# A two-layer hybrid decoder trunk: setup joined with the first layer, modulation sums by block turns, and the last norm turned and scaled by rows

## The chip, the cores and the metric

The kernel runs on one core of one Trainium2 chip. The metric is the device time of one execution in microseconds (us). A profiled execution gives, beside its time, a trace of every engine: TensorE (PE, with its weight loads as PEld), VectorE (DVE), ScalarE (ACT), GpSimd (POOL), SyncE (SP) and the DMA queues.

## What is computed

The reference, cut to what matters here (512 tokens, width 1024, two layers, all in float32):

```python
c_act = jax.nn.silu(c)
for l in range(DEPTH):
    mod = c_act @ ada_w[l] + ada_b[l]                      # 1024 -> 9 * 1024
    sh1, sc1, g1, sh2, sc2, g2, sh3, sc3, g3 = jnp.split(mod, N_MOD, axis=-1)
    h = modulate(rms_norm(x, ffn1_norm[l]), sh1, sc1)      # y * (1 + sc) + sh
    x = x + 0.5 * g1[:, None, :] * swiglu(h, ffn1_w_in[l], ffn1_w_out[l])
    h = modulate(rms_norm(x, mix_norm[l]), sh2, sc2)
    ...                                                    # attention and convolution branches
    x = x + g2[:, None, :] * (merged @ w_mix_out[l])
    h = modulate(rms_norm(x, ffn2_norm[l]), sh3, sc3)
    x = x + 0.5 * g3[:, None, :] * swiglu(h, ffn2_w_in[l], ffn2_w_out[l])
return rms_norm(x, final_norm)
```

The attention adds a bias that depends on the distance of two tokens (a table of 8 heads by 32 buckets) and uses a scalar lambda per layer, made of four vectors of 64.

## The kernel before

x is kept in SBUF with channels on the partitions: 8 tiles (j) of 128 channels by 512 tokens (`x_res`). Each matrix product is done in float32 accuracy with three reduced-precision products: a weight slab of 128 output channels is loaded by SP (`w_raw`, `slab`, L285), rounded by ACT (`w_hi_part`, L390), its rest taken by DVE (`w_lo_part`, L680), and PE runs, for each of its 8 (or 6) chunks, three matmuls of 512 columns, high by high, high by low, low by high (`slab`, L1205). There are two slots for slabs. The order of the work on each engine is written out by hand, and semaphores tie the engines together.

**Norms.** A norm's scale per token is not known when the product with x can start. So a stage's first two slabs (`two_slabs`, L1220) are multiplied with x times a per-channel scale, without the token's factor, and their result is scaled afterwards (`read_bank` in `norm_units`, L722); two columns with the shift are multiplied in the same pass (L1240, L1241). Meanwhile PE sums the squares over channels (`norm_mean`, L1263, a matmul with a constant matrix), ACT takes the root (L396) and DVE the reciprocal (L692). `norm_units` then makes the 8 normed tiles on DVE and ACT, and the second pair of slabs and all later ones use those.

**Modulation.** The product of the activated c with `ada_w` runs on DVE, beside the matmuls: for each chunk of 1024 outputs, 8 weight tiles of 128 by 1024 are multiplied by one scalar per partition and added (`ada_step`, L784). What is left is a sum over the 128 partitions. `chunk_parts` (L797) splits the 128 by 1024 sum into a high and a low part, `mod_sum_parts` (L1275) adds over partitions with four matmuls of 512 columns, `mod_rows` (L804) copies the two rows out, `mod_turn` (L1285) turns them into columns with four float32 matmuls, which the trace shows as eight, and `mod_columns` (L810) adds `ada_b`. There are 16 such chunks, 8 in input stages of feed-forward networks (ffn), 8 in output stages; POOL's queue loads their weights (`ada_chunk`, L356).

**Setup (L293 to L484, L828 to L880, L1293 to L1329).** The first two chunks of layer 0 (shift and scale of the first norm) come as 8 loads of 1 MB on POOL's queue into `ada_first`. SP loads x by rows and 16 small parameter rows, then the first weight slabs. ACT's queue issues the loads of c, convolution taps, bias table and eight broadcasts of the lambda vectors, before ACT activates c (L450). PE turns x tile by tile (L1302), ACT copies and squares each tile, DVE adds the squares. Eight rows of the attention bias are made, one per head, each replicated over 128 partitions (L1316, L1317), copied (L468, L469) and written to HBM (L472). PE then adds the first chunks over partitions (L1271) and turns them (L1289), DVE makes the scale and shift columns, and the first norm's pass starts (L1237).

**End.** In the last ffn's output stage (L953 to L978) each of 8 channel tiles takes three slabs; DVE updates x (L776), ACT squares it (L435), DVE adds the square (L782). After the last tile follow the mean over channels (L1261), root, reciprocal of 128 by 512 (L694), 8 times a scaled tile (L1199), four PE turns (L1502) and an ACT copy (L673), and eight stores of 256 KB (L333), the second four behind the last copy.

## Time and profile before

| | us |
|---|---|
| time, median of 3 runs | 2619.57 (2619.23 to 2621.32) |
| time of the profiled execution | 2620.49 |
| its span in the trace | 2618.7 |
| PE busy | 2558.0 (98%) |
| DVE busy | 1669.3 (64%) |
| ACT busy | 973.8 (37%) |
| POOL busy | 101.3 (4%) |

The profiled execution is 0.92 us over the median of the runs, and its own span is 1.8 us shorter than its time. PE's busy time counts every moment in which some matmul is in flight; matmuls overlap, so a full PE is read from the pitch between their starts. A float32 matmul stands in the trace as two.

### The profile page before, as it was taken

How to read it: one execution, taken by the hardware profiler on the slowest of the kernel's cores; microseconds unless marked ns; L12 is line 12 of the kernel's file. 1: busy time of each engine (PE TensorE's matmuls, PEld its weight loads, DVE VectorE, ACT ScalarE, POOL GpSimd, SP SyncE). 2: the span in 40 equal slices, each digit the busy share in tenths (PEclk: the TensorE clock that was granted, in tenths of full speed). 3: DMA queues.
4: the chain of work that ended last, by engine and by line, in shares of the span. 5: the costliest groups of instructions: out<-in, count | busy, mean ns of one | idle time of the engine just before them, and what ended most of it. 6: DMA issues, size and time to landing. Idle time of an engine off the chain costs nothing.

```text
span 2618.7 us, 34873 instructions
## 1 busy us (share of the span) xinstructions
PE 2558.0 (98%) x11578; PEld 2059.3 (79%) x11578; DVE 1669.3 (64%) x2449; ACT 973.8 (37%) x1637; POOL 101.3 (4%) x163
## 2 busy tenths in 40 slices
PE   4999999999999999999999999999999999999997
PEld 2688888777778888888878888877777788788886
DVE  3655567789898666544365556678898875633333
ACT  2422222554554433222232222244554453422222
POOL 0000001000000000000000001101000000000000
PEclk9999999999999999999999999999999999999998
DMA  6355556232223344543324556632222333333332
GB/s 225 113 156 160 160 185 216 77 88 84 80 84 90 94 125 122 159 128 92 96 85 139 150 159 195 222 101 85 80 84 80 93 93 93 91 96 97 98 95 92
DMA packets 469953, 311.96 MB, mean 119 GB/s; under 512 B 11047, under 2 KB 447529, under 8 KB 468872
## 3 DMA queue, kind: packets, MB, share of 16 engines
q1 hardware_dynamic: 445260, 227.69, 29.8%
q0 software_dynamic: 19584, 75.51, 8.5%
q10 hardware_dynamic: 5052, 8.02, 1.0%
q8 instruction: 34, 0.56, 0.1%
q14 instruction: 23, 0.19, 0.0%
HBM read 306.13 MB, written 5.05 MB: 119 GB/s over the span
## 4 chain that ended last, share of the span: by engine, by line
PE 93%; DVE 4%; ACT 1%; ACTq 1%; issue 1%; DVEq 0%
PE bank L1215 28%; PE bank L1217 27%; PE bank L1216 27%; PE bank L1413 2%; PE bank L1392 1%; PE bank L1242 1%; ACTq L446 1%; PE bank L1237 1%; PE bank L1238 1%; DVE rstd L694 1%; PE bank L1384 1%; DVE w_lo L683 1%; PE bank L1289 1%; DVE scaled L705 1%; PE bank L1316 1%
## 5 line engine op out<-in xcount | busy, mean ns | idle before, releaser
L683 DVE TENSOR_TENSOR w_lo<-w_raw,w_hi 128x1024 fp32r<-128x1024 f32 (+1 forms) x434 | 522.4, 1204 | 578.2 <-ACT w_hi L394 577.6
L1215 PE MATMUL bank<-h_hi,w_hi 128*128 128x512 f32 x2112 | 838.7, 397 | 0.0
L1217 PE MATMUL bank<-h_hi,w_lo 128*128 128x512 f32 x2112 | 823.8, 390 | 0.0
L1216 PE MATMUL bank<-h_lo,w_hi 128*128 128x512 f32 x2112 | 822.2, 389 | 0.0
L394 ACT ACTIVATE w_hi<-w_raw 128x1024 fp32r<-128x1024 f32 (+1 forms) x434 | 451.7, 1041 | 878.3 <-PE bank L1217 866.8
L1215 PEld LDWEIGHTS bank<-h_hi,w_hi 128*128 128x128 f32 x2112 | 396.5, 188 | 89.7 <-issue 8.2
L1217 PEld LDWEIGHTS bank<-h_hi,w_lo 128*128 128x128 f32 x2112 | 396.4, 188 | 84.6
L1216 PEld LDWEIGHTS bank<-h_lo,w_hi 128*128 128x128 f32 x2112 | 397.0, 188 | 77.9 <-issue 0.5
L1005 DVE SCALAR_TENSOR_TENSOR conv_part<-glu,conv_taps,conv_part 128x512 f32<-128x512 f32 x464 | 318.9, 745 | 0.0
L1215 PE MATMUL bank<-s_hi,w_hi 128*128 128x512 f32 x704 | 274.6, 390 | 0.0
L1217 PE MATMUL bank<-s_hi,w_lo 128*128 128x512 f32 x704 | 274.0, 389 | 0.0
L1216 PE MATMUL bank<-s_lo,w_hi 128*128 128x512 f32 x704 | 273.9, 389 | 0.0
L1215 PEld LDWEIGHTS bank<-s_hi,w_hi 128*128 128x128 f32 x704 | 132.1, 188 | 27.7
L1217 PEld LDWEIGHTS bank<-s_hi,w_lo 128*128 128x128 f32 x704 | 132.1, 188 | 27.5
L1216 PEld LDWEIGHTS bank<-s_lo,w_hi 128*128 128x128 f32 x704 | 132.2, 188 | 27.4
L793 DVE SCALAR_TENSOR_TENSOR ada_acc<-ada_raw,c_act,ada_acc 128x1024 f32<-128x1024 f32 x112 | 143.4, 1280 | 0.9
L364 POOL DMA_DIRECT2D ada_raw<-in_ada_w x128 | 67.9, 531 | 1270.2 <-DVE ada_acc L790 575.2
L513 ACT ACTIVATE s_hi<-full 128x512 f32 (+1 forms) x84 | 53.1, 632 | 166.3 <-DVE full L916 166.3
L918 DVE TENSOR_TENSOR s_lo<-full,s_hi 128x512 f32 (+1 forms) x84 | 58.2, 693 | 75.3 <-ACT s_hi L513 75.3
L435 ACT ACTIVATE squares<-x_res 128x512 f32 x48 | 30.3, 632 | 197.3 <-DVE x_res L776 197.3
L569 ACT ACTIVATE probs<-probs,neg_row_max 128x512 f32<-128x512 f32 (+3 forms) x128 | 71.0, 556 | 76.7 <-DVE neg_row_max L1042 76.6
L782 DVE TENSOR_TENSOR running_sum<-running_sum,squares 128x512 f32<-128x512 f32 x56 | 38.8, 692 | 78.8 <-ACT squares L435 44.1
(182 smaller groups left out, 2642.3 us busy)
## 6 DMA issues: line engine op xcount, KB each, us to landing
w_raw<-in_ffn_w_in SPq DMA_DIRECT2D x176, 512.0 KB, 3.8
ada_raw<-in_ada_w POOLq DMA_DIRECT2D x128, 512.0 KB, 4.7
w_raw<-in_w_mix_in SPq DMA_DIRECT2D x112, 512.0 KB, 3.6
w_raw<-in_ffn_w_out SPq DMA_DIRECT2D x64, 512.0 KB, 3.9
w_raw<-in_ffn_w_out SPq DMA_DIRECT2D x32, 384.0 KB, 3.4
w_raw<-in_w_mix_out SPq DMA_DIRECT2D x18, 512.0 KB, 3.8
ada_first<-in_ada_w POOLq DMA_DIRECT2D x8, 1024.0 KB, 24.3
w_raw<-in_w_attn_branch SPq DMA_DIRECT2D x16, 512.0 KB, 3.8
```

The lines of the kernel that those rows point to most:

```text
L364: pool.dma_start(ada_raw[k % 4][:, :], w_ada[:, ds(layer * KT + k, 1), ds(m * D, D)].rearrange("p o f -> p (o f)"))\
L394: act.activation(whi[slot][:, 0:n, :], raw[slot][:, 0:n, :], ACT.Copy).then_inc(w_hi[slot], 1)
L513: act.activation(tile(SHI2, i), F[0][:, :], ACT.Copy).then_inc(sem("s_hi"), 1)
L569: act.activation(PR[par][m][:, 0:n], PR[par][m][:, 0:n], ACT.Exp, bias=nmx[:, par, m:m + 1], scale=-1.0, accum_out=rsum[:, par, m:m + 1]). ...
L683: dve.tensor_tensor(wlo[slot][:, 0:n, :], raw[slot][:, 0:n, :], whi[slot][:, 0:n, :].bitcast(F32), ALU.subtract).then_inc(w_lo[slot], 1)
L793: ins = dve.scalar_tensor_tensor(out=ACC[:, :], in0=ada_raw[k % 4][:, :], scalar=CA[:, k:k + 1], in1=ACC[:, :], op0=ALU.mult, op1=ALU.add)
L918: dve.tensor_tensor(tile(SLO2, i), F[0][:, :], tile(SHI2, i).bitcast(F32), ALU.subtract)\
L1005: ins = dve.scalar_tensor_tensor(out=CAB[t % 2][:, :], in0=Z[:, t:t + TOK], scalar=wt, in1=CAB[t % 2][:, :], op0=ALU.mult, op1=ALU.add)
L1215: pe.matmul(acc, wh, hi[:, k0 + k, :], start=first and k == 0, stop=False)
L1216: pe.matmul(acc, wh, lo[:, k0 + k, :], start=False, stop=False)
L1217: mm = pe.matmul(acc, wl, hi[:, k0 + k, :], start=False, stop=last and k == n - 1)
L1413: mm = pe.matmul(S[m][:, 0:n], QT[m * HD:(m + 1) * HD, i * P:(i + 1) * P], KTT[m * HD:(m + 1) * HD, 0:n], start=True, stop=True)
```

## The change

- `ada_w`'s first 2 MB by 4 are loaded in two halves, the scale's 8 tiles first; the shift's 8 tiles and the lambda broadcasts follow on POOL's queue once the first two weight slabs have landed. SP loads the small rows before x.
- All bias rows come from one pair of matmuls (16 partitions per head) and are written by eight stores, issued by ACT after it has made the first high parts.
- The squares of x are summed along x's rows by ACT, and put into `running_sum` as scaled columns of the identity matrix.
- The first pass of slabs starts when the scale is known. Its shift columns are multiplied after it (`late`), the mean of squares at its ninth step.
- Each chunk's sum over partitions is made by turning 32 by 32 blocks on DVE, a reduction of each block's rows on DVE, and one float32 matmul of 32 columns; four small additions give the columns.
- In the last stage, x times `final_norm` is turned tile by tile between slabs, squares are summed per token by matmuls of one column, and at the end row blocks are scaled once and stored in four stores of 512 KB. The last stage's loop is written out.
- The lambda sums and exponentials move behind the first norm and the first ffn's input stage.

```diff
-    TBX = at("table_wide", [P, HEADS, P], F32, s0 + 4256)
+    TBX = at("table_wide", [P, HEADS, P // HEADS], F32, s0 + 4256)
@@ block.sync
-        for t in range(QB):
-            sp.dma_start(XS[:, t, :], a["x"][0, t * P:(t + 1) * P, :]).then_inc(sem(f"x_in{t}"), 16)
         for l in range(DEPTH):
...
+        for t in range(QB):
+            sp.dma_start(XS[:, t, :], a["x"][0, t * P:(t + 1) * P, :]).then_inc(sem(f"x_in{t}"), 16)
...
+        for n in range(QB):
+            t = n // 2 + 2 * (n % 2)
+            sp.wait_ge(sem(("y_scaled_dve", "y_scaled_act")[n % 2]), n // 2 + 1)
+            sp.dma_start(out[0, t * P:(t + 1) * P, :], YO[:, t, :]).then_inc(sem("y_out"), 16)
@@ block.gpsimd
         for k in range(KT):
-            pool.dma_start(ADA0[:, k, :], w_ada[:, k, 0:2 * D]).then_inc(sem(f"ada0_in{k}"), 16)
+            pool.dma_start(ADA0[:, k, D:2 * D], w_ada[:, k, D:2 * D]).then_inc(sem(f"ada0_scale{k}"), 16)
+        for s in range(2):
+            pool.wait_ge(w_raw[s], 16)
+        for k in range(KT):
+            pool.dma_start(ADA0[:, k, 0:D], w_ada[:, k, 0:D]).then_inc(sem(f"ada0_shift{k}"), 16)
+        for l in range(DEPTH):
+            for n, name in enumerate(("lambda_q1", "lambda_k1", "lambda_q2", "lambda_k2")):
+                pool.dma_start(LV[:, l, n, :], bass.AP(a[name].tensor, l * HD, [[0, P], [1, HD]]))\
+                    .then_inc(sem("lambda_in"), 16)
@@ block.scalar
+        act.activation(BR[:, 0:TOK], TP[1][:, :], ACT.Copy).then_inc(sem("br_copied"), 1)
+        act.activation(BR[:, TOK:TOK + P], TP[0][:, 0:P], ACT.Copy).then_inc(sem("br_copied"), 1)
         for j in range(KT):
             act.wait_ge(sem("xp_ready"), j + 1)
             act.activation(X[:, j, :], bank[2 + j % 2][:, :], ACT.Copy).then_inc(sem("x_ready"), 1)
-            act.wait_ge(sem("ssum_add"), j)
-            act.activation(SQ[:, :], bank[2 + j % 2][:, :], ACT.Square).then_inc(sem("sq_ready"), 1)
+        for t in range(QB):
+            act.activation(JUNK[t % 2][:, :], XS[:, t, :], ACT.Square, accum_out=row_sq[:, t:t + 1])...
...
         for s in range(2):
             w_hi_part(0, s)
+        for t in range(QB):
+            act.activation(SSUM[:, t * P:(t + 1) * P], ident[:, :], ACT.Copy, scale=row_sq[:, t:t + 1])...
         for j in range(KT):
             plain_hi(0, j)
+        for c in range(HEADS):
+            act.dma_start(bass.AP(src.tensor, src.offset + c * (P // HEADS) * (TOK + P),
+                          [[P * (TOK + P), HEADS], [TOK + P, P // HEADS], [1, TOK + P]]), BR[:, :])...
@@ block.vector
         def chunk_parts(seq):
             dve.wait_ge(sem("ada_step"), (seq + 1) * KT)
-            dve.tensor_copy(ACCH[:, :], ACC[:, :]).then_inc(sem("acc_hi"), 1)
-            dve.wait_ge(sem("acc_hi"), seq + 1)
-            dve.tensor_tensor(ACCL[:, :], ACC[:, :], ACCH[:, :].bitcast(F32), ALU.subtract).then_inc(sem("acc_parts"), 1)
+            dve.transpose(ACCT[:, :], ACC[:, :]).then_inc(sem("acc_turned"), 1)
+            dve.wait_ge(sem("acc_turned"), seq + 1)
+            dve.wait_ge(sem("mod_summed"), seq + 1)
+            dve.tensor_reduce(RED[:, :], ACCT[:, :].rearrange("p (b r) -> p b r", r=32), AX.X, ALU.add)\
+                .then_inc(sem("acc_parts"), 1)
+        def chunk_columns(layer, hc, turn):
+            dve.wait_ge(sem("mod_summed"), turn + 1)
+            for q in range(4):
+                quarter = slice(q * 32, (q + 1) * 32)
+                ins = dve.tensor_tensor(MODC[quarter, ...], O[quarter, q:D // 32:4], PT[quarter, ...], ALU.add)
+            ins.then_inc(sem("modc_ready"), 1)
...
         for k in range(KT):
+            first_step(1, "scale", k)
+        first_parts(1, 0)
...
+        w_lo_part(0, 0)
+        w_lo_part(0, 1)
+        dve.wait_ge(sem("scale0_summed"), 1)
+        quarter_columns(KT).then_inc(sem("scale0_ready"), 1)
         scale_columns(0, 0).then_inc(sem("ac_ready"), 1)
-        shift_columns(0, 0)
         for j in range(KT):
             plain_lo(0, j)
+        for k in range(KT):
+            first_step(0, "shift", k)
+        first_parts(0, 1)
+        dve.wait_ge(sem("mod_summed"), 1)
+        quarter_columns(0).then_inc(sem("modc_ready"), 1)
+        shift_columns(0, 0)
...
+        dve.tensor_copy(YO[:, :, j * P:(j + 1) * P], TP[j % 2]...)
+        dve.reciprocal(yrstd[:, :], yroot[:, :]).then_inc(sem("y_rstd"), 1)
+        for t in (0, 1):
+            dve.tensor_scalar(YO[:, t, :], YO[:, t, :], yrstd[:, t:t + 1], None, ALU.mult)...
@@ block.tensor
+            if late:
+                pe.wait_ge(sem("scale0_ready"), 1)
+                first_sum(1).then_inc(sem("mod_summed"), 1)
+                pe.wait_ge(sem("shift_parts"), 2)
+                for slot in range(2):
+                    for n in range(KT):
+                        wh, wl = whi[slot][:, n, :], wlo[slot][:, n, :]
+                        pe.matmul(S[slot][:, 0:2], wh, SHP[:, shift, n, :], start=n == 0, stop=False)
+                        mm = pe.matmul(S[slot][:, 0:2], wl, SHP[:, shift, n, :], start=False, stop=n == KT - 1)
+                    mm.then_inc(w_used[slot], 1)
+        def turn_rows(j):
+            pe.wait_ge(sem("y_gained"), j + 1)
...
+            for t in range(QB):
+                mm = pe.transpose(TP[j % 2][:, t * P:(t + 1) * P], T[j % 2][:, t * P:(t + 1) * P], ident[:, :])
+        def token_sums():
+            for t in range(QB):
+                pe.matmul(AUX[:, t:t + 1], SSUM[:, t * P:(t + 1) * P], invd[:, 0:1], start=t == 0, stop=False)
         def mod_sum_parts(turn):
-            for r in range(2):
-                one = SELR[:, ROWS_MAX - 1 - r:ROWS_MAX - 1 - r + 64]
-                pe.matmul(O[0:64, :], one, ACCH[:, r * TOK:(r + 1) * TOK], start=(r == 0), stop=False)
-                mm = pe.matmul(O[0:64, :], one, ACCL[:, r * TOK:(r + 1) * TOK], start=False, stop=(r == 1))
+            pe.matmul(O[:, 0:D // 32], SELG[:, :], RED[:, :], start=True, stop=True).then_inc(sem("mod_summed"), 1)
-        def mod_turn(turn, rows):
-            for q in range(4):
-                mm = pe.matmul(O[:, q:4 * rows:4], MR[0:64, q * P:(q + 1) * P], ident[0:64, 0:rows], ...)
```

## Rows read from the trace of the kernel before

**Rows 1.** Page, part 4: the chain that ended last, by engine

```profile
PE 93%; DVE 4%; ACT 1%; ACTq 1%; issue 1%; DVEq 0%
```

**Rows 2.** Timeline, 0 to 110 us: start, duration, engine, line, operation, count, wait before

```profile
9.21 20.39 SPq L287 DMA_DIRECT2D w_raw<-in_ffn_w_in  x2
...
16.19 1.33 PE L1302 MATMUL bank<-ident,x_rows 128*128 128x128 f32 x5 [4.82 <-DMA x_rows<-in_x]
...
19.66 3.68 ACTq L446 DMA_DIRECT2D lambda_rows<-in_lambda_k  x1
...
23.85 10.61 ACTq L446 DMA_DIRECT2D lambda_rows<-in_lambda_k  x1
...
43.85 1.12 PE L1302 MATMUL bank<-ident,x_rows 128*128 128x128 f32 x4 [0.24 <-ACT squares L456]
...
78.73 0.77 PE L1237 MATMUL bank<-h_hi,w_hi 128*128 128x512 f32 x1 [3.85 <-DVE h_lo L771]
...
86.63 3.35 DVE L694 RECIPROCAL rstd<-rstd 128x512 f32<-128x512 f32 x1 [3.15 <-ACT rstd L401]
...
95.79 1.22 DVE L683 TENSOR_TENSOR w_lo<-w_raw,w_hi 128x1024 fp32r<-128x1024 f32 x1
...
109.47 0.47 PE L1215 MATMUL bank<-h_hi,w_hi 128*128 128x512 f32 x1
```

**Rows 3.** The tile ada_first's eight loads: time from issue to landing

```profile
DMA to landing us min/median/max: 11.0/24.3/35.1
```

**Rows 4.** Windows: stretch, length, PE, PEld, DVE, ACT, POOL, PEclk, DMA share, GB/s

```profile
25.00:30.00 5.00, 0.00 (x0) 0.00 (x0) 0.00 (x0) 0.00 (x0) 0.00 (x0) 1.00 1.02 388
...
82.00:86.00 4.00, 4.00 (x10) 2.59 (x10) 1.48 (x6) 0.16 (x1) 0.00 (x0) 0.55 0.91 264
86.00:90.00 4.00, 4.00 (x25) 3.43 (x23) 3.35 (x1) 0.53 (x1) 0.00 (x0) 1.00 0.03 10
```

**Rows 5.** Page, part 5: groups, with busy time and mean ns of one

```profile
L394 ACT ACTIVATE w_hi<-w_raw 128x1024 fp32r<-128x1024 f32 (+1 forms) x434 | 451.7, 1041 | 878.3 <-PE bank L1217 866.8
...
L793 DVE SCALAR_TENSOR_TENSOR ada_acc<-ada_raw,c_act,ada_acc 128x1024 f32<-128x1024 f32 x112 | 143.4, 1280 | 0.9
```

**Rows 6.** Timeline around one chunk's sum and turn, ffn input stage

```profile
170.71 1.22 DVE L802 TENSOR_TENSOR ada_acc_lo<-ada_acc,ada_acc_hi 128x1024 fp32r<-128x1024 f32 x1
...
174.85 0.39 PE L1281 MATMUL bank<-ada_acc_hi,row_select_r 128*64 128x512 f32 x1
...
175.76 0.39 PE L1215 MATMUL bank<-h_hi,w_hi 128*128 128x512 f32 x1
...
186.41 0.39 PE L1217 MATMUL bank<-h_hi,w_lo 128*128 128x512 f32 x1
...
188.04 0.40 PE L1216 MATMUL bank<-h_lo,w_hi 128*128 128x512 f32 x1
```

**Rows 7.** Timeline of PE: one turn (at 552) and a mean (at 464) between matmuls

```profile
552.25 0.39 PE L1217 MATMUL bank<-h_hi,w_lo 128*128 128x512 f32 x1
...
552.82 0.39 PE L1216 MATMUL bank<-h_lo,w_hi 128*128 128x512 f32 x1
...
464.17 0.48 PE L1242 MATMUL bank<-h_hi,w_lo 128*128 128x512 f32 x1
...
465.57 0.39 PE L1238 MATMUL bank<-h_lo,w_hi 128*128 128x512 f32 x1
```

**Rows 8.** Timeline around one chunk's sum, ffn output stage

```profile
422.64 0.69 DVE L800 CAST ada_acc_hi<-ada_acc 128x1024 fp32r<-128x1024 f32 x1
423.37 1.23 DVE L802 TENSOR_TENSOR ada_acc_lo<-ada_acc,ada_acc_hi 128x1024 fp32r<-128x1024 f32 x1
...
424.88 0.39 PE L1281 MATMUL bank<-ada_acc_hi,row_select_r 128*64 128x512 f32 x1
```

**Rows 9.** Timeline of the end

```profile
2597.32 0.75 DVE L776 SCALAR_TENSOR_TENSOR x_res<-bank,gates,x_res 128x512 f32 x1 [1.93 <-PE bank L1217]
...
2610.84 5.21 SPq L333 DMA_DIRECT2D out<-y_rows  x8
```

More of the change, by code:

```diff
@@ L1218, in slab, with two_slabs @@
             mm.then_inc(w_used[slot], 1)
[L1220 removed]
+        def two_slabs(pair, use, ready, shift=None, at={}, banks=G, late=False):
             lag = 4
@@ L1238, in two_slabs @@
                     pe.matmul(acc, wh, HLO[:, n, :], start=False, stop=False)
-                    if shift is not None:
+                    if shift is not None and not late:
                         pe.matmul(S[slot][:, 0:2], wh, SHP[:, shift, n, :], start=n == 0, stop=False)
@@ L1368, in _ @@
                              k0, OUTG[g], g == 0, g == 2,
-                             at={2: lambda: mod_sum_parts(seq + 1)} if w == 0 and m == 5 else {})
-                    if w == 0:
-                        mod_turn(seq + 1, 2)
+                             at=extra.get(m, {}))
+                if last:
+                    for i in range(KT // 2):
+                        out_pair(i)
+                else:
+                    with pe.Fori(0, KT // 2) as i:
+                        out_pair(i)
                 if w == 1:
```

351 lines of the change are left out of this document (191 added, 160 removed).

## The prediction

> **What bounds the kernel now.** I read the chain of waits first: 93% of the path that ended last is PE [rows 1]. Inside the stages PE takes a 512-column matmul every 0.2275 us: four of them in 0.91 us [rows 6]. So two kinds of time can be won: matmuls that are not the product itself, and the two ends in which PE waits. The timeline of the start shows the first: the pass of the first norm begins at 78.73 us, and only at 109.47 us do the plain slabs begin [rows 2]. The first 35 us go to ACT's queue, which is stuck in issuing lambda loads (the last takes 10.61 us, to 34.5), so c is not activated before that. The timeline of the end shows the second: the last update of x starts at 2597.32 us of a span of 2618.7, 21.4 us from the end [rows 9]. Between them, 16 chunk sums interrupt PE.
>
> **The chunk sums.** Removed on PE, per chunk: four matmuls, 0.91 us, and the turn. Around the turn two matmul starts that are normally 0.455 us apart stand 188.04 - 186.41 = 1.63 us apart [rows 6], so it costs 1.18 us. Together 2.09 us. Added: one float32 matmul of 32 columns, two in the trace. The trace has none of this form. The nearest rows are a single 128-column turn, which stretches two starts from 0.455 to 0.57 us, so 0.12 us, and the mean with two float32 passes of 512 columns, 1.40 - 0.455 = 0.95 us [rows 7]. I take 0.3 us, twice the turn's price and a little for the start, since the short form is much nearer to the turn. Per chunk 1.8 us, for 16 chunks 29 us; by the ends 31.5 and 18.2 us.
>
> On DVE, a copy of 0.69 us and a subtraction of 1.23 us, 1.95 us with the gap [rows 8], give way to a block turn and a reduction of 128 by 1024. Neither operation is in the trace. The cheapest pass of that width is the copy, 0.69 us; the dearest DVE operation is the reciprocal, 3.35 us for 512 columns, 6.7 us for 1024 [rows 2]. Most passes of that width take 1.2 to 1.3 us [rows 5, 8]. I take 1.2 us for each, since both read every column once: 2.4 us, 0.5 us more than now. In the input stage the low part ends at 171.93 and PE asks at 174.85 [rows 6], so 2.9 us of other matmuls hide it. In the output stage it ends at 424.60 and PE asks at 424.88 [rows 8]: only 0.28 us. There PE will wait some 0.25 us in each of 8 chunks, 2 us. The row copy that goes and the four small additions that come lie on neither path; behind them on DVE stands the next slab's low part, which is early there. Net gain of this part: 27 us.
>
> The Trainium skill (VectorE: DVE Perf Modes, The perf-mode tier table) states that the reduction runs in the slowest mode, one element per cycle, and (Vector Engine (DVE) Microarchitecture Reference, The reshape front-end and per-opcode configuration) that the block turn also sustains one element per cycle. By both the pair would take an estimated 2.2 us, and PE's wait in the output stage would all but vanish; no row here shows either.
>
> **The setup.** ACT's queue keeps only six issues, so c is active before 10 us and this delay is gone. What comes next? *Transfers.* The start moves data at 388 GB/s [rows 4]. Before the shift half come 4.2 MB of scale weights, 2.1 MB of x, 1.05 MB of slabs and 0.3 MB of taps and tables: 20 us of full rate. But x is now issued behind the 16 small rows, just ahead of the slabs' issue at 9.21 us, where before it landed by 16.2 us [rows 2], and it shares the rate with the scale loads. With half the rate it needs 11 us from about 8.5; the last load of a group also lags (one took 35.1 us from its issue [rows 3]). I put x's landing at 25 us (20 to 27) and the last scale tile at 31.
>
> *The chain from x.* Eight tiles turn at 1.1 us (the 1.12 us of four turns [rows 2]), and the copy ends at 34.5. ACT then squares four rows of 1024 columns (1.04 us each as its own pass of that width [rows 5], and some 0.1 for the sum read out): 39.1; taps 39.8; high parts of both slabs 41.9. DVE's second low part ends at 43.1 (1.22 us), four additions and the scale column at 44. Then one high part (0.65), one low part (0.7), and PE's first matmul stands at 45.5 us, against 78.73. The scale's own chain is shorter: its last step at 31 + 1.3, turn, reduction and matmul by 36, hidden behind ACT.
>
> *The chain of the shift.* This is where gain is given back. DVE's eight low parts end at 50.2 (0.7 us each, a little under the 0.75 us of a like pass [rows 9], since passes overlap). Only then does it start on eight shift steps, 0.7 + 7 x 1.28 = 9.7 us [rows 5]: 59.9. Their loads are issued once the slabs have landed, about 35, and need 11 us: hidden. Turn and reduction 62.3, PE's matmul and the columns 63.7. In the same DVE order stands the reciprocal, which before began at 86.63. PE has ended its pass by 60, 16 matmuls at about 0.43 and 32 at 0.23 us plus the mean; it waits until 62, does the sum and, at 64, 32 shift matmuls in some 4 us, and waits again: the second pass needs a low part that stands 10.4 us behind the reciprocal's start (95.79 + 1.22 - 86.63 [rows 2]), so it starts at 74.2. From the reciprocal's start to the plain slabs it was 109.47 - 86.63 = 22.8 us; the lambda sums, now in between on DVE, add 0.8: 87.4.
>
> At 74.2 PE comes from some 6 idle us. After such a stretch before the first pass, the granted clock was 0.55 between 82 and 86 us and 1.00 between 86 and 90 [rows 4], that is 1.2 GHz at first and 2.4 GHz then; the first pass began at 78.73, so some 7 us went at 1.2 GHz. I charge 5 to 7 us at half speed, which puts 48 matmuls at 13 to 14.5 us and the plain slabs at 88.2. The Trainium skill (TensorE: Matmul & The Clock Gate, HAM oscillation) says that an idle stretch sends the clock back to half; this trace agrees, with the 0.55 just named. With a clock that stayed up DVE's chain would decide, and the plain slabs would stand at 87.4. Gain of the setup: 109.47 - 88.2 = 21.3 us. Its bounds: x by 20 us gives 26; by 27 us and a second pass wholly at half speed (48 x 0.43 = 20.6 us from 76) gives 13.
>
> The 8 stores of bias rows are costed at nothing: ACT issues them from 50 us on, and its next task, the root, is wanted at 60. If that cover goes, the second rival below has the price. Chunk loads on POOL's queue wait for the lambda sums, at 82; the first of them is wanted when the first chunk's tile begins, near 98: hidden. SP's slabs of the second pair are issued at 41 and share the rate with the shift loads until 50; they are wanted at 70.
>
> **The end.** Added to PE in the last stage: seven groups of four turns at four times 0.12 us [rows 7], 3.4 us, and four float32 matmuls of one column, eight in the trace, at no more than the removed turn's 1.18 us [rows 6], 1.0. ACT's products and copies (half a slab's 1.04 us [rows 5] and a little, 0.6 us each) lie in its idle time; the slab behind them is needed a whole slab later. After PE's last matmul, taken as 0: x updated at 1.0; square 1.85; column sums 3.0; last product by ACT 2.4, turned 3.8; a dummy high part and a copy keep ACT until 3.9, the root is there at 4.3; DVE's dummy low part ends at 4.7, the last copy 5.4, the reciprocal of four columns 5.6. Scaling: DVE 6.3 and 7.0, ACT 6.7 and 7.7. The first store's data flows from 7.7, 2.1 MB at 388 GB/s [rows 4] take 5.4 us, and the end comes at 14. Now it is 21.6 us (0.25 us from PE's last matmul to 2597.32, then 21.4). Gain 7.6 - 4.4 = 3 us, between -2 and 6.
>
> **Sum.** 27 + 21.3 + 3 = 51.3 us off the profiled execution's 2620.5: 2569.2. The median of the runs is 0.9 lower: 2568. A change of 0.2%, about 5 us, is what a measurement of this kernel can tell from none.
>
> **Rivals.** (1) *The block turn is slow on DVE.* If it costs what the reciprocal does per column (6.7 us, with the reduction 7.9, 6.0 more than now), PE waits 6.0 - 2.9 = 3.1 us in 8 input-stage chunks and 5.7 in 8 output-stage ones, 70 us in all, and 5.5 more in the shift's chain. Against 53.3 us of gain without waits this gives 2619.6 + 22 = 2642: slower. It decides from a block turn of about 5.4 us on. For it: a turn over partitions is no ordinary pass. Against: no other DVE row here is as slow per column as the reciprocal. The page on the microarchitecture named above speaks against it. Chance 4%.
>
> (2) *ACT is caught in issuing stores.* Eight stores back to back on its queue, as the lambda loads were, of which the last two took 3.68 and 10.61 us to issue [rows 2]. At 3.5 us each ACT is free at 78 instead of 53; the root then is 19 us later, the reciprocal at 79.5 instead of 63.8, and 15.7 us of the setup's gain are gone: 2584. For it: the same queue, 128 packets each. Against: those loads were issued while the queues moved 388 GB/s [rows 4]; by 50 us most loads have landed. Chance 14%.
>
> (3) *The sum matmul costs as much as a mean* (0.95 us), and DVE's pair is half a us longer than I think: 18.2 - 6 = 12 us instead of 27: 2583. Chance 12%.
>
> (4) *The early start does not come*, because the slabs land as late as 41 us, as the 35.1 us of the slowest load of the start allow [rows 3]: ACT's high parts end at 43 and the shift loads flow until 58; the plain slabs begin near 91: 2571, inside the forecast's range. The part that would not do what it says is the shift, which ends up as long as all of the old setup; at most 21 us, 2589. Chance of the latter 4%.
>
> **Numbers.** Forecast case 66%, on its own 2556 to 2579; the rivals 14, 12, 4 and 4%. The range of 2554 to 2587 takes in the rivals at 2583 and 2584 and the faster bounds of clock, x and matmul. Faster by over 0.2%: 94%; within 0.2%: 2%; slower: 4%.
>
> **What would show it.** First matmul of the first norm near 45.5 us; plain slabs near 88; between them two gaps on PE, 60 to 62 and 68 to 74, with a low granted clock behind the second. Chunk pairs in the output stage about 1.6 us shorter, each with a short PE wait on the reduction; input-stage groups 1.8 us shorter with no wait. Block turn and reduction near 1.2 us each. Last matmul to the end 14 us. Wrong would be: PE waiting for the reduction by more than 0.5 us, ACT's root behind store issues, or x landing after 30 us.

## The result, and where the time went

The kernel after took 2576.5 us (median of 4 runs, 2575.4 to 2577.8), the kernel before 2619.4 beside it (2618.6 to 2621.3): ratio 0.9835, 95% interval 0.9818 to 0.9852. The forecast was 2568, its range 2554 to 2587. The sum was 51.3 us of gain, and 42.9 came. The profiled execution took 2577.0 us, its span is 2575.3.

An update of x is the same instruction in both kernels, so the difference of its start times cuts the gain into parts. First the updates of the kernel before, from the timeline of DVE (start, duration, engine, line, operation, tiles, idle time before it), the first of the first output stage and the first of the last one:

```profile
349.46 0.75 DVE L776 SCALAR_TENSOR_TENSOR x_res<-bank,gates,x_res 128x512 f32 x1
...
2492.62 0.75 DVE L776 SCALAR_TENSOR_TENSOR x_res<-bank,gates,x_res 128x512 f32 x1 [1.94 <-PE bank L1217]
```

And those of the kernel after, with the last update of all (before, it is the first line of [rows 9]):

```profile
327.18 0.74 DVE L810 SCALAR_TENSOR_TENSOR x_res<-bank,gates,x_res 128x512 f32 x1
...
2453.25 0.75 DVE L810 SCALAR_TENSOR_TENSOR x_res<-bank,gates,x_res 128x512 f32<-128x512 f32 x1 [1.70 <-PE bank L1292]
...
2562.38 0.75 DVE L810 SCALAR_TENSOR_TENSOR x_res<-bank,gates,x_res 128x512 f32<-128x512 f32 x1 [2.64 <-PE bank L1292]
```

The lead is 22.3 us at the first of them and 39.4 at the second. At the last it is only 2597.32 - 2562.38 = 34.9: the last stage gives 4.4 back. At the end of the span it is 43.4. With the plain slabs' start (109.47 in [rows 2], 92.03 below) the gain splits into **setup 17.4, chunk sums 21.9, end 4.0** (8.5 behind the last update, less 4.4). The forecast had 21.3, 27 and 3.

**The setup.** The timeline of the kernel after, 20 to 92 us:

```profile
22.62 0.47 PE L1399 MATMUL bank<-ident,x_rows 128*128 128x128 f32 x1 [14.55 <-DMA x_rows<-in_x]
...
30.10 0.48 PE L1399 MATMUL bank<-ident,x_rows 128*128 128x128 f32 x1 [3.18 <-DMA x_rows<-in_x]
...
31.96 4.48 PE L1399 MATMUL bank<-ident,x_rows 128*128 128x128 f32 x21 [1.38 <-DMA x_rows<-in_x]
35.44 4.18 POOL L355 DMA_DIRECT2D ada_first<-in_ada_w  x8 [29.25 <-DMA w_raw<-in_ffn_w_in]
49.06 0.77 PE L1312 MATMUL bank<-h_hi,w_hi 128*128 128x512 f32 x1 [9.63 <-DVE h_lo L805]
...
66.62 0.61 PE L1375 MATMUL bank<-ada_group_sums,group_select 128*128 128x32 f32 x2 [3.77 <-DVE ada_group_sums L846]
...
68.27 3.35 DVE L728 RECIPROCAL rstd<-rstd 128x512 f32<-128x512 f32 x1
...
78.87 0.77 PE L1312 MATMUL bank<-h_hi,w_hi 128*128 128x512 f32 x1 [3.47 <-issue]
...
92.03 0.47 PE L1290 MATMUL bank<-h_hi,w_hi 128*128 128x512 f32 x1
```

The four tiles of x land one by one, the last at 31.95 us and not at 25. PE's first matmul stands at 49.06 (forecast 45.5, before 78.73), the reciprocal at 68.27 (63.8), the second pass 10.6 us behind it (10.4), the plain slabs at 92.03 (88.2). The windows of the kernel after (stretch, length, PE, PEld, DVE, ACT, POOL busy, PEclk, DMA share, GB/s) hold the reason for x and a second surprise:

```profile
25.00:30.00 5.00, 0.47 (x1) 0.18 (x1) 2.13 (x2) 0.00 (x0) 0.00 (x0) 1.00 0.34 103
30.00:35.00 5.00, 3.52 (x15) 2.62 (x16) 3.62 (x3) 1.80 (x3) 0.00 (x0) 1.00 0.14 42
...
70.00:75.00 5.00, 5.00 (x25) 5.00 (x25) 4.73 (x6) 1.48 (x3) 0.00 (x0) 0.50 0.00 0
75.00:80.00 5.00, 1.53 (x5) 1.29 (x6) 4.93 (x8) 3.12 (x4) 0.00 (x0) 0.50 0.00 1
```

PE, ACT and POOL wait for loads from 25 us on (PE and ACT up to 32, POOL up to 35.44), and yet the sixteen DMA engines are a third, then a seventh busy. And the clock is at its lower level, 1.2 GHz, from 70 to 80 us, in the first half of it with PE never idle: the 32 shift matmuls of 2 columns took 7.0 us where I had put 4.

**The chunk sums.** In the input stage, the timeline of PE in the kernel after: the sum's two matmuls between plain ones, and, 11 us later, the loop's turning point:

```profile
157.17 0.40 PE L1292 MATMUL bank<-h_hi,w_lo 128*128 128x512 f32 x1
157.40 0.31 PE L1381 MATMUL bank<-ada_group_sums,group_select 128*128 128x32 f32 x2
157.54 0.48 PE L1290 MATMUL bank<-h_hi,w_hi 128*128 128x512 f32 x1
157.86 0.39 PE L1291 MATMUL bank<-h_lo,w_hi 128*128 128x512 f32 x1
...
168.29 0.39 PE L1292 MATMUL bank<-h_hi,w_lo 128*128 128x512 f32 x1
168.70 0.47 PE L1290 MATMUL bank<-h_hi,w_hi 128*128 128x512 f32 x1
169.00 0.39 PE L1291 MATMUL bank<-h_lo,w_hi 128*128 128x512 f32 x1
```

From 157.17 to 157.86 are two steps, normally 0.455, so the sum costs 0.24 us (forecast 0.3). From 168.29 to 169.00 it is 0.26 more than two steps, with nothing in between: here PE's loop over the chunks starts over. At its second turn, at 234.11, it is 0.3 more; where the loop ends, at 300.01, only 0.1. Before, the modulation turn stood at this very place ([rows 6], up to 188.04), and any such time was part of its 1.18 us. In the output stage:

```profile
368.26 1.22 DVE L837 TENSOR_REDUCE ada_group_sums<-ada_acc_turned 128x32 f32<-128x1024 f32 x1
...
368.87 0.39 PE L1292 MATMUL bank<-s_hi,w_lo 128*128 128x512 f32 x1
...
369.53 0.41 PE L1381 MATMUL bank<-ada_group_sums,group_select 128*128 128x32 f32 x2 [0.27 <-DVE ada_group_sums L837]
...
370.09 0.40 PE L1291 MATMUL bank<-s_lo,w_hi 128*128 128x512 f32 x1
```

PE could go on at 369.10, the reduction ends at 369.48: from 368.87 to 370.09 is 1.22 us, 0.77 over two steps. Less the 0.24 of the sum itself, 0.53 go to the wait (0.38 up to the end of the reduction) and to the start behind it. The period of a pair there (two channel tiles and one chunk) is 30.73 us (32.06 before), that of a group of six tiles with one chunk in the input stage 65.86 (67.42).

**The end.** The timeline of the kernel after, behind the last update at 2562.38:

```profile
2563.16 0.63 ACT L454 ACTIVATE squares<-x_res 128x512 f32<-128x512 f32 x1 [4.68 <-DVE x_res L810]
...
2565.45 1.22 DVE L717 TENSOR_TENSOR w_lo<-w_raw,w_hi 128x1024 fp32r<-128x1024 f32 x1 [2.33 <-ACT w_hi L401]
2566.60 0.68 DVE L1268 COPY y_rows<-bank 128x512 f32<-128x512 f32 x1
2567.41 0.18 DVE L1272 RECIPROCAL y_rstd<-y_root 128x4 f32<-128x4 f32 x1
...
2568.41 2.90 SPq L333 DMA_DIRECT2D out<-y_rows  x4
```

A reciprocal of 4 columns, 0.18 us, does what 3.35 us did, and 12.9 us lie between the last update and the end, where 21.4 lay in [rows 9].

### The profile page after: what moved, and what is told of

It reads as the page before. It is cut to its first block, busy times and chain, and to the rows that moved or that the text cites. A ratio compares the mean times of both kernels' runs of the same rounds, so it can differ in the third digit from the quotient of the medians.

```text
span 2575.3 us, 34488 instructions
## 1 busy us (share of the span) xinstructions
PE 2509.5 (97%) x11392; PEld 2032.6 (79%) x11392; DVE 1671.7 (65%) x2488; ACT 972.7 (38%) x1635; POOL 108.7 (4%) x177
## 4 chain that ended last, share of the span: by engine, by line
PE 85%; DVE 8%; ACT 3%; issue 2%; DMA 1%; SPq 0%; ACTq 0%; DVEq 0%
PE bank L1290 26%; PE bank L1292 26%; PE bank L1291 26%; PE bank L1513 2%; DVE ada_acc L827 1%; PE bank L1492 1%; ACT w_hi L401 1%; DVE rstd L728 1%; DMA x_rows<-in_x 1%; DVE w_lo L717 1%; DVE scaled L739 1%; PE bank L1312 1%; PE bank L1484 1%; DVE h_lo L748 1%; PE bank L1313 1%
## 5 line engine op out<-in xcount | busy, mean ns | idle before, releaser
L1290 PE MATMUL bank<-h_hi,w_hi 128*128 128x512 f32 x2112 | 838.9, 397 | 1.6 <-DVE scaled L963 1.3
L454 ACT ACTIVATE squares<-x_res 128x512 f32 (+1 forms) x48 | 30.4, 633 | 194.4 <-DVE x_res L810 194.4
L1312 PE MATMUL bank<-h_hi,w_hi 128*128 128x512 f32 x192 | 81.6, 425 | 17.1 <-DVE h_lo L805 9.6
```

What stands on the lines that cost most here:

```text
L1290: pe.matmul(acc, wh, hi[:, k0 + k, :], start=first and k == 0, stop=False)
L1312: pe.matmul(acc, wh, HHI[:, n, :], start=n == 0, stop=False)
```

## Experiments

The times are medians of 5 runs (of 4 in experiment 7), to be set against 2576.5. The same code moves by about 1 us between executions, so what is smaller is read in the traces, and a trace is one execution too: five kernels with the same setup, but for a few small instructions (the kernel after and those of experiments 5 to 8), have their plain slabs at 91.89 to 93.30 us.

**1. x first.**

```
+        for t in range(QB):
+            sp.dma_start(XS[:, t, :], a["x"][0, t * P:(t + 1) * P, :]).then_inc(sem(f"x_in{t}"), 16)
         for l in range(DEPTH):
             rows = [("ffn1_norm", KT), ("mix_norm", KT), ("ffn2_norm", KT), ("conv_dw_bias", KT),
...
-        for t in range(QB):
-            sp.dma_start(XS[:, t, :], a["x"][0, t * P:(t + 1) * P, :]).then_inc(sem(f"x_in{t}"), 16)
```

> The kernel after, with the four loads of x issued ahead of the 16 small rows on SP's queue. In the kernel after x lands at 31.95 us. Theory A (the forecast's: the end of the setup hangs on x through ACT and the order on DVE): x lands at 20 to 24 us, the first matmul moves from 49.06 to about 44, and the plain slabs from 92.03 to about 87: 5 us faster, 2571.5. Theory B (the shift's loads are next: POOL issues them only when the two slabs have landed, at 35.4, and DVE's last shift step already waited for its tile until 62.65): x lands early and the first matmul moves, but the shift steps end no earlier than 63.5, the plain slabs stand at 91.5 or later, and the time is within 1 us of 2576.5.

2568.5 us, 8.1 faster. x had landed by 11.9 us, and the plain slabs stood at 83.56. Theory A holds, by more than it said: the setup hangs on x, and the shift's loads (the shift steps now run from 44.7 to 55.2) were not next. The timeline and windows of this kernel show what was:

```profile
11.86 6.92 PE L1399 MATMUL bank<-ident,x_rows 128*128 128x128 f32 x32
...
30.50 1.91 PE L1408 MATMUL bank<-ident,tap_rows 31*128 31x31 f32 x16 [4.40 <-DMA tap_rows<-in_conv_dw]
...
34.26 4.17 POOL L355 DMA_DIRECT2D ada_first<-in_ada_w  x8 [28.06 <-DMA w_raw<-in_ffn_w_in]
```

```profile
25.00:30.00 5.00, 0.67 (x2) 0.29 (x2) 2.17 (x2) 0.00 (x0) 0.00 (x0) 0.50 0.06 25
30.00:35.00 5.00, 1.91 (x16) 1.78 (x16) 4.11 (x5) 2.56 (x5) 0.74 (x2) 0.50 0.05 15
```

The 31 rows of taps land only now, at 30.5 us, and up to then the DMA share is 0.06: one engine of sixteen, at 25 GB/s, while DVE waits for scale tiles and POOL for the slabs.

**2. Taps behind x.**

```
-        for l in range(DEPTH):
-            act.dma_start(CWR[0:CK, l, :], a["conv_dw"][l, :, :]).then_inc(sem("taps_in"), 16)
...
         act.activation(BR[:, TOK:TOK + P], TP[0][:, 0:P], ACT.Copy).then_inc(sem("br_copied"), 1)
+        for t in range(QB):
+            act.wait_ge(sem(f"x_in{t}"), 16)
+        for l in range(DEPTH):
+            act.dma_start(CWR[0:CK, l, :], a["conv_dw"][l, :, :]).then_inc(sem("taps_in"), 16)
```

> The kernel after, with the two tap loads (31 partitions, 124 KB each) issued on ACT's queue only when x has landed. Theory C (the taps pass through one of the 16 DMA engines or few, and x, the scale tiles and the slabs each have a part behind them there: between 25 and 35 us the DMA share is only 0.34 and 0.14, while the tiles of x land 3.2 to 3.8 us apart): without them x lands at 21 to 24 us instead of 31.95, the slabs by 26 instead of 35.4, so that the shift's loads start 9 us earlier too; the taps land 10 us after x, about 33, and ACT's high parts stand at 35 to 36; first matmul 41 to 42, plain slabs 84 to 85, 7 to 8 us faster: 2569. Theory D (x is late because it is issued late and shares the rate): the taps are 0.25 MB, 0.6 us at 388 GB/s; x lands at 31 or later, the taps after it delay ACT, and the time is 2577 to 2585.

2576.9 us, no difference, and yet theory C holds in its first half. The timeline of this kernel:

```profile
20.83 6.01 PE L1401 MATMUL bank<-ident,x_rows 128*128 128x128 f32 x29 [0.82 <-DMA x_rows<-in_x]
...
24.77 4.16 POOL L355 DMA_DIRECT2D ada_first<-in_ada_w  x8 [18.60 <-DMA w_raw<-in_ffn_w_in]
...
41.06 1.91 PE L1410 MATMUL bank<-ident,tap_rows 31*128 31x31 f32 x16 [14.02 <-DMA tap_rows<-in_conv_dw]
43.54 2.00 ACT L401 ACTIVATE w_hi<-w_raw 128x1024 fp32r<-128x1024 f32 x2
```

x is there at 20.83 instead of 31.95, the slabs at 24.77 instead of 35.44: 11 us, for 0.25 MB that were moved away. 248 KB at the 25 GB/s of one engine are 10 us. Theory D, by which the same bytes were 0.6 us, is out. What the expectation missed: the taps then took 20 us, most likely because their engine also carried its share of the shift's loads, which were issued 4 us behind them; and ACT's high parts stand behind the tap copies in its order. The gain was lost to the next wait in the same chain.

**3. Taps in 124 partitions.** The same bytes as 124 rows of 1 KB, two transposes and a rearranging copy for each layer.

```
-            act.dma_start(CWR[0:CK, l, :], a["conv_dw"][l, :, :]).then_inc(sem("taps_in"), 16)
+            act.dma_start(CWR[0:4 * CK, l, :], a["conv_dw"][l, :, :].rearrange("k (q c) -> (k q) c", q=4)).then_inc(sem("taps_in"), 16)
...
-            for h in range(HEADS):
-                mm = pe.transpose(G[l][:, h * CK:(h + 1) * CK], CWR[0:CK, l, h * P:(h + 1) * P], ident[0:CK, 0:CK])
+            for b in range(2):
+                mm = pe.transpose(G[l][:, b * 4 * CK:(b + 1) * 4 * CK], CWR[0:4 * CK, l, b * P:(b + 1) * P], ident[0:4 * CK, 0:4 * CK])
```

> The kernel after, with each tap load in 124 partitions of 1 KB rows instead of 31 of 4 KB, turned by two matmuls instead of eight; it stays where it was on ACT's queue. Theory C (the load of 31 partitions goes through one DMA engine, which the tiles of x, scale and slabs all need; the run with the taps behind x had x at 20.83 us and the slabs at 24.8, but the taps themselves only at 41.06): x lands at 20 to 23 us, the slabs by 27, the taps before both; ACT's high parts start near 32, first matmul near 38, plain slabs near 81 instead of 92: 11 us faster, 2565.5. Theory E (the spread load is slow too, or the tap turn and copies get dearer): x at 26 or later, and 0 to 6 us faster. Theory F (the early part moves, but ACT, issuing its eight stores of bias rows while the shift loads flow, has the root late): first matmul near 38, the root behind the shift steps' end, and less than 8 us faster.

2571.6 us, 4.9 faster; x at 25.52, plain slabs at 86.67. Between C and E: against the kernel with the taps away x still loses 4.7 us, where 31 rows cost it 11.1. The Trainium skill (DMA: Bandwidth & Descriptors, Why a DMA increments its semaphore by 16 and not by 1, the paragraph How many engines) says that a DMA is split over the largest number of engines, up to 16, that divides the slowest dimension of both its sides: which makes one for 31 rows, four for 124, sixteen for 128. The share of 0.06 in experiment 1 agrees with the one; the two delays agree in their order, though 4.7 is more than a quarter of 11.1.

**4. Both, and the later sum.** The edits of experiments 1, 3 and 5 together.

> The kernel after, with three edits: taps in 124 partitions, x issued first on SP's queue, the output stage's chunk sum three K tiles later. If C holds: x at 12 us as with x first alone, scale by 20 and slabs by 25, high parts from 23, first matmul near 30, shift steps from 34 to 45, plain slabs near 73, 19 us before those of the kernel after; with the 3.1 to 3.6 us of the later sum: 2554. If the shift's loads (4.2 MB, 11 us at 388 GB/s, issued at 25 beside the second slabs and the bias-row stores) are next: plain slabs at 75 to 78 and 2556 to 2559. If the taps are still what ACT waits for (30.5 us with x first alone): about 2565.

2557.4 us, 19.1 faster than the kernel after. Plain slabs at 76.61, 15.4 earlier; the sum gave the rest. Read at the same place, x first alone gave 8.5 (83.56) and the spread taps alone 5.4 (86.67): together they give 1.6 more than their sum, little beyond the 1.4 by which equal setups differ. That each alone leaves the chain to the other wait is seen in the traces: with x first ACT waits for the taps up to 32.45, with the taps spread x lands at 25.52 only.

**5. The sum three K tiles later.**

```
-                        extra[5] = {2: lambda: mod_sum_parts(seq + 1)}
+                        extra[5] = {5: lambda: mod_sum_parts(seq + 1)}
```

> The kernel after, with the chunk sum of the output stage three K tiles later in the same slab (nine matmuls, 2.0 us). In the kernel after, the output stage's pair period is 30.73 us against 29.92 for 132 matmuls at 0.2267: 0.81 per chunk, of which the sum's own slot is 0.24 by the input stage, and PE asks some 0.4 us before the reduction ends. Theory A: the wait goes, the period is 30.2, 8 chunks times 0.55: 4.4 us faster, 2572.1. Rival: the extra is no wait for the reduction but the restart of PE at a changed kind of matmul, or the wait turns up at DVE's small additions behind the slab: the period stays within 0.1 us of 30.73 and the time within 1 us of 2576.5.

2573.4 us, 3.1 faster by the medians. The pair period is now 30.17 (341.94 to 372.11), 0.56 less in each of 8 chunks, 4.5 us in all: theory A. The profile has no wait for the reduction left. Its plain slabs stood 0.6 us later than those of the kernel after (92.66), in the same code, which the total has lost.

**6. The old chunk sums in the kernel after.** DVE's copy and subtraction, PE's four matmuls and the turn, as before; setup and end stay.

> The kernel after with the chunk sums of the kernel before (copy and subtraction on DVE, four matmuls and the turn on PE; the setup and the end stay new). By the stretches between updates of x in the two traces this part gave 21.9 us, which would make it 2598.4. By the forecast it gave 27 us: 2603.5. Less than 20 would mean that part of what the stretches show belongs to the setup or to the norms' entries.

2598.4 us, 21.9 slower than the kernel after: the part's price by the stretches, but not to the tenth. In the profiled executions 21.7 us lie between the two, and 1.3 of them came before the plain slabs (93.30), in the setup that this edit hardly touches: the sums themselves cost 20.4 there. 8 chunks of the input stage at 1.56 and 8 of the output stage at 1.33 would be 23.1; see below for the rest.

**7. The old end in the kernel after.**

> The kernel after with the end of the kernel before: no turns or token sums in the last stage; mean, root and reciprocal over 512 columns, product, turn and copy tile by tile, eight stores. By the stretches of the two traces the new end costs 4.4 us in the last stage and saves 8.5 behind the last update of x, 4.0 in all: 2580.6. By the forecast 3 us: 2579.6. A difference under 2 or over 6 us would mean that the two ends interact with something else.

2582.6 us (4 runs), 6.1 slower. Its trace has 104.7 us from the first to the last update of the last stage (109.1 in the kernel after, so 4.4 is what the new end costs there) and 22.2 from the last update to the end (12.9). That makes 4.8; the rest of the 6.1 lies in the stretches ahead of the last stage, where the two kernels are the same, by 0.8 in the profiled executions. So 4 to 6 us for the new end.

**8. The tail without unused slab parts.**

```
-                        w_lo_part(p + 1, m % 2, OUTG[(m + 2) % 3] if m < 4 else 8)
+                        if not (last and i == KT // 2 - 1 and m >= 4):
+                            w_lo_part(p + 1, m % 2, OUTG[(m + 2) % 3] if m < 4 else 8)
```

ACT's high parts get the same condition, and the two loads behind them go.

> The kernel after without the slab parts that nobody uses at the end: the last two loads of w_raw, high parts and low parts. In the kernel after DVE's low part (1.22 us from 2565.45) stands in front of the copy of the last tile (2566.60), whose turn was done near 2565.7, and ACT's high part stands in front of a copy and the root. Theory A (both are on the path that ends last): from the last update of x to the end 12.92 becomes 12.0 us, 0.9 us faster. Rival (the stores' transfers decide, 339 GB/s in the last 5 us, or the root does): less than 0.3 us in that stretch. By the medians alone this is near what cannot be told.

From the last update (2563.80) to the end (2576.0) are 12.2 us instead of 12.9: most of what theory A said. The median, 2577.7, does not show it. In the profiled execution the first update of x came 0.9 us later than in the kernel after (granted clock 0.51 from 80 to 85 us, where that has 0.65) and another 0.5 was lost before the last stage, in the same code: more than what the edit gives. It is kept for its trace alone.

**9. A warm PE, first try.** Ten float32 matmuls that nobody reads, in PE's waits of the first norm.

> The kernel after, with ten float32 matmuls of 512 columns that nobody reads (running_sum by inv_d into the second pass's first bank, which that pass clears) in PE's waits around the first norm's shift: three before the sum, one behind it, four behind the shift matmuls, two more once three low parts are done. In the kernel after the granted clock is 0.50 to 0.65 between 65 and 85 us; the 32 shift matmuls take 7.0 us and the second pass 13.16 us from 78.87. Theory A (the clock costs little, since DVE's ladder ends at 86.93 whatever PE does): the clock stays near 1.00, the shift matmuls take about 3.5 us, the second pass still begins at 78.9, and the plain slabs move from 92.03 to 91 at most: 0 to 1 us faster. Theory B (PE at 1.2 GHz binds the second pass): plain slabs at 89.8, 2.2 us faster. Third case: the clock falls all the same, the idle-time matmuls run at 1.9 us each and PE is late: the plain slabs stand 5 us or more later.

2577.5 us, no difference: the third case in part. The shift matmuls, begun at a clock of 1.00, took 3.7 us instead of 7.0, but the clock fell before they were through: the last two steps between them are 0.21 us, the others 0.11 (granted 0.70 from 70 to 75, 0.62 from 75 to 80). The last fillers made the second pass 1.7 us late, at 80.58, and it then ran at full speed to 91.88.

**10. A warm PE, second try.** The same, with four of the fillers among the shift matmuls.

```
                         mm = pe.matmul(S[slot][:, 0:2], wl, SHP[:, shift, n, :], start=False, stop=n == KT - 1)
-                    mm.then_inc(w_used[slot], 1)
+                        if n % 4 == 3:
+                            if n == KT - 1:
+                                mm.then_inc(w_used[slot], 1)
+                            pe.matmul(TP[0][:, :], invd[:, :], SSUM[:, :], start=True, stop=True)
```

> The kernel after with ten float32 matmuls of 512 columns that nobody reads, placed otherwise than in the first try: three before the first norm's sum, one behind it, one after every eighth of the 32 shift matmuls, two behind them. In the first try the clock was 1.00 up to 72 us, but fell during the matmuls of 2 columns, so that the fillers behind them took 1.8 us each and the second pass began at 81.1 instead of 78.9. Theory A (wide matmuls in between hold the clock): granted clock 0.95 or more from 65 to 85 us, second pass from 78.9 at a pitch of 0.23, plain slabs at 90 to 90.6, DVE's last low part at 86.9 being what holds them; 1.5 us faster. Rival (the clock falls in any case): fillers at 1.8 us each, second pass at 80 or later, plain slabs at 92 or later.

2576.8 us, no difference. The windows of this kernel:

```profile
70.00:75.00 5.00, 5.00 (x31) 3.75 (x30) 4.73 (x6) 1.38 (x2) 0.00 (x0) 1.00 0.00 1
75.00:80.00 5.00, 3.53 (x10) 1.64 (x10) 4.93 (x8) 3.23 (x4) 0.00 (x0) 1.00 0.00 0
80.00:85.00 5.00, 4.56 (x20) 3.03 (x19) 4.93 (x8) 2.17 (x3) 0.00 (x0) 1.00 0.65 190
```

The clock stayed at 2.4 GHz, and the plain slabs moved from 92.03 to 91.41 only. Its timeline shows why:

```profile
82.72 0.39 PE L1317 MATMUL bank<-h_hi,w_lo 128*128 128x512 f32 x1
83.42 0.50 PE L1312 MATMUL bank<-h_hi,w_hi 128*128 128x512 f32 x1 [0.31 <-DVE h_lo L748]
```

A fast PE waits for DVE's low parts. Theory A holds for the clock, not for the 1.5 us: in this pair of traces 0.6 us were gained, which is less than equal setups differ by (experiment 7, without fillers, has its plain slabs at 91.89). So the clock at 1.2 GHz costs the setup little here, and how little these runs don't show.

**11. The small root.** Edits 1, 3, 5 and 8, and the first norm's root and reciprocal taken on the 128 by 4 row sums, as at the end.

```
+        act.activation(row_root[:, :], row_sq[:, :], ACT.Sqrt, bias=eps[:, 0:1], scale=1.0 / D).then_inc(sem("row_root"), 1)
...
-            act.activation(SSUM[:, t * P:(t + 1) * P], ident[:, :], ACT.Copy, scale=row_sq[:, t:t + 1]).then_inc(sem("row_sums"), 1)
+            act.activation(SSUM[:, t * P:(t + 1) * P], ident[:, :], ACT.Copy, scale=row_rstd[:, t:t + 1]).then_inc(sem("row_sums"), 1)
...
-            root(l * AUXN + AUX_NORM[k], l * UNITS + UNIT_NORM[k])
+            if l == 0 and k == 0:
+                act.wait_ge(sem("aux_ready"), 1)
+                act.activation(RSTD[:, :], AUX[:, :], ACT.Copy, scale=float(D)).then_inc(sem("aux_read"), 1)
+            else:
+                root(l * AUXN + AUX_NORM[k], l * UNITS + UNIT_NORM[k])
...
+        dve.reciprocal(row_rstd[:, :], row_root[:, :]).then_inc(sem("rstd_ready"), 1)
```

> The three edits of the 2557.4 us kernel (taps in 124 partitions, x first, later sum), the short end without unused slab parts, and one more: the first norm's root and reciprocal are taken on the 128 by 4 row sums (0.18 us as at the end) before they are spread over the bank, and DVE's reciprocal of 512 columns (3.35 us, at 53.05 there) goes. Theory A (DVE's order behind the shift binds up to the second pass): the second pass starts 3.3 us earlier, at 60.3, plain slabs at 73.3 instead of 76.6; with 0.7 at the end 4.0 us faster: 2553.4. Rival (the 32 shift matmuls at 1.2 GHz are next: they end near 60.2, and slot 1's high part and DVE's reading of the second bank wait for them): plain slabs at 74.5 or later, 2 us or less from this edit: 2555.

**2552.0 us** (2551.0 to 2553.4), ratio to the kernel before 0.9743, interval 0.9730 to 0.9756: the fastest of all, 24.5 us under the kernel after. The timeline of the kernel:

```profile
60.27 0.35 PE L1344 MATMUL bank<-shift_parts,w_lo 128*128 128x2 f32 x1
61.04 0.77 PE L1324 MATMUL bank<-h_hi,w_hi 128*128 128x512 f32 x1 [0.41 <-issue]
...
73.42 0.47 PE L1302 MATMUL bank<-h_hi,w_hi 128*128 128x512 f32 x1
```

Plain slabs at 73.42, 3.2 earlier, by theory A; but the second pass now stands right behind the last shift matmul, so the rival is next. One more row, from the timeline of ACT:

```profile
38.46 8.12 ACTq L499 DMA_DIRECT2D bias_rows<-bias_row  x2
46.63 0.60 ACT L424 ACTIVATE rstd<-bank 128x512 f32<-128x512 f32 x1 [9.51 <-issue]
```

The last two stores of bias rows hold ACT for 8.1 us while the shift's loads flow.

**12. Small root and warm PE.** Eight fillers, and none among or behind the last eight of the 32 shift matmuls.

> The 2552.0 us kernel with the unread float32 matmuls in PE's waits of the first norm: four before the sum, one behind it, and one after every eighth shift matmul but the last (three). In that kernel the 32 shift matmuls ran at 1.2 GHz, ended at 60.5 and held the second pass, which began at 61.04 and ended at 73.42. Theory A (PE is what binds there now, so that the clock has a price, other than in the kernel after): granted clock near 1.00 from 50 to 70 us, shift matmuls and fillers end near 60.4, second pass from 60.5 at full speed; DVE's last low part then holds it, plain slabs near 72: 1.0 to 1.8 us faster, 2550.6. Rival (DVE's order binds there too): plain slabs at 73.2 or later and no difference, 2552.

2554.9 us, 2.9 slower than experiment 11 (2.4 in the profiled executions): both theories missed. The windows:

```profile
55.00:60.00 5.00, 4.51 (x29) 3.41 (x27) 4.90 (x7) 3.26 (x5) 0.00 (x0) 0.99 0.25 100
60.00:65.00 5.00, 4.39 (x10) 3.51 (x11) 4.96 (x8) 2.06 (x3) 0.00 (x0) 0.50 0.37 109
```

The clock held up to 60 us and had fallen when the second pass began (at 60.60), behind eight bare shift matmuls, still 0.11 us apart, and 1.1 idle us. The pass then ran its first part at 1.2 GHz and ended at 74.50, 1.1 later. What the fall hangs on isn't settled by these runs: in experiment 10 three fillers and 1.5 idle us followed the last shift matmul and the clock held, here no filler did. The other 1.3 us came after the first update of x, in the same code.

## Why the forecast held, and where its steps failed

Time and direction were right, at the slow side of the range: 2576.5 against 2568. The three parts were off by 5.1, 3.9 and 1.0 us, the last one to the other side. Of the three signs of being wrong that the prediction names, x did land behind 30 us; ACT's root did stand behind the store issues, but with time to spare; and PE's wait for the reduction, 0.38 us up to its end and 0.53 with the start behind it, is at the bound of 0.5. By its own steps:

- **Chunk sums, 27 forecast, 21.9 measured.** What the turn and the four matmuls cost, 2.09 us, was right; what took their place was not. In the input stage the start of the loop, which had been a part of the turn's 1.18 us, became 0.26 us of its own: 2.09 - 0.24 - 0.26 = 1.59, and the period says 1.56. In the output stage the wait was forecast at 0.25 us and is 0.53 with the start behind it: 2.09 - 0.24 - 0.53 = 1.32, and the period says 1.33. "2.4 us, 0.5 us more than now" was right (1.25 + 1.22, against 1.95), but 0.5 us more behind a cover of 0.28 leaves a wait of 0.2 to 0.4 and the start again behind it. The rest, 23.1 less 21.9, is lost between the stages, where the norms' entries stand; in the first of them two starts of PE are 0.94 us apart instead of 0.23 (449.34 to 450.28), and the profile puts the idle time down to issue. Its cause was not followed further and stays open.
- **Block turn and reduction.** 1.25 and 1.22 us against 1.2 each. The estimate from two pages of the Trainium skill (VectorE: DVE Perf Modes, The perf-mode tier table; Vector Engine (DVE) Microarchitecture Reference, The reshape front-end and per-opcode configuration) was 2.2 us for the pair and hardly a wait; the trace has 2.47 and a wait. Rival 1 is out.
- **The sum matmul.** 0.24 us where I took 0.3; rival 3 is out.
- **x's landing, 25 forecast (20 to 27), 31.95 measured.** This is the step whose reasoning failed; as a date it was off by most, 7 us, though in the sum it cost less than the chunk sums did. The sentence "4.2 MB of scale weights, 2.1 MB of x, 1.05 MB of slabs and 0.3 MB of taps and tables: 20 us of full rate" counts bytes over sixteen engines. The taps go through one, and everything that needs that engine queues with them: 11.1 us by experiment 2, and not the 0.6 that 248 KB cost at the full rate. The other half is the order: with x issued first it had landed by 11.9 us in spite of the taps (experiment 1). The mark was there in the trace of the kernel before, in this window:

```profile
40.00:45.00 5.00, 4.28 (x18) 2.75 (x18) 2.53 (x4) 3.93 (x8) 0.00 (x0) 1.00 0.06 16
```

A share of 0.06 is one engine of sixteen; most likely it is the same two loads of taps, for which nobody was waiting there. The spread of [rows 3], 11.0 to 35.1 us, which I read as a group's last load lagging, says less: 8 MB at 388 GB/s alone are 21.6 us. Of the 7 us, 3.6 reached the first matmul, since the eight turns and copies behind the last tile took 6.4 us (31.95 to 38.4) where I had put 9.5.
- **The DVE chain.** From the first matmul to the reciprocal 19.2 us against 18.3, from there to the second pass 10.6 against 10.4, to the plain slabs 23.8 against 24.4. Eight low parts, eight shift steps, turn, sum: in that order and of those lengths. This is what experiments 1, 4 and 11 pull on, and it moves nearly whole each time.
- **The clock.** "5 to 7 us at half speed" was 4.7 (78.87 to 83.6). The shift matmuls ran at half speed as well, 7 us and not 4, hidden behind DVE. "With a clock that stayed up DVE's chain would decide, and the plain slabs would stand at 87.4", 0.8 earlier: experiment 10 has 0.6, within what equal setups differ by, and does show the wait for DVE.
- **ACT's stores.** Rival 2 had the mechanism and not the price. The timeline of ACT in the kernel after:

```profile
52.08 6.42 ACTq L494 DMA_DIRECT2D bias_rows<-bias_row  x5
58.53 1.28 ACT L405 ACT_TABLE_LOAD   x1 [6.20 <-issue]
...
60.13 0.69 ACT L408 ACTIVATE rstd<-bank,eps 128x512 f32<-128x512 f32 x1
```

ACT is free at 58.5, root and all at 60.8, and DVE asks for it at 68.27: 7.5 us of cover. That the root "is wanted at 60" was the date at which it could run, and not the one at which DVE asks. In experiment 11 the same stores took ACT 8.1 us for two.
- **The end, 3 forecast, 4.0 by the stretches (4 to 6 by experiment 7).** Added: 4.4 of 4.4. A group of four turns made the half pair 15.46 us instead of 14.96, seven times. From PE's last matmul to the end 13.2 us against 14.
- **Rival 4** foresaw the slabs at 41 us; they came at 35.44, and x was the later cause. Its 2571 lay nearer to the result than the forecast, with the right culprit (one load that lands late) at the wrong tile.

## What to carry to other kernels

Cost a load not by its bytes but by the bytes on the busiest DMA engine: two loads of 31 partitions, issued while the loads that the first matmul needs were under way, made these land 11 us later here, and a low DMA share while several engines wait for loads is their mark. When two waits guard one chain, take both away before you judge either: the edits alone moved the plain slabs by 8.5 and 5.4 us, together by 15.4. Price a removed step by the difference to the same place without it, not by the whole gap around it; and a scalar for each token is worth computing on 4 columns before it is spread over 512.

## What the runs showed of the hardware

- While two loads of 31 partitions were under way, the DMA share fell to 0.06, that of one engine of sixteen, at 25 GB/s, and the last tiles of 128 partitions came in one by one (experiment 1, 25 to 30 us). In the same way the tiles of x, 128 partitions each, landed up to 3.8 us apart in the kernel after, with a DMA share of 0.34 and then 0.14 from 25 to 35 us.
- 32 matmuls of 2 columns, back to back, left PE "5.00 of 5.00 us busy" and the granted clock at 0.50 all the while (70 to 75 us): it was down when they began, behind 3.8 and 1.2 idle us, and they did not bring it back. Begun at 1.00 it fell before the last of them (experiment 9). With 512-column float32 matmuls among them it stayed at 1.00 (experiment 10). Issue to issue they took 0.21 us at 1.2 GHz and 0.11 at 2.4.
- The second pass of the same code, started cold at 78.9 to 79.7 us, came up to full speed near 83.6 us in the kernel after and near 85 in experiments 6 and 8. That fits a part of the 1 us by which executions of the same code differ.
